# Two transformer blocks with a mixture of experts on one core: the overflow loop between the 16th and 17th expert, and expert outputs added to x in memory

## What is computed

```python
def hierarchical_moe(h, w_rg, b_rg, w_re, b_re, w_gate, w_up, w_down):
    ...
    expert_ids = g_idx[:, None] * EXPERTS_PER_GROUP + top_idx      # two experts a token
    combine = ...                                                  # its two weights
    out = jnp.zeros_like(tok)
    for e in range(N_EXPERTS):
        hid = jax.nn.silu(tok @ w_gate[e]) * (tok @ w_up[e])       # 1024 -> 256
        out = out + combine[:, e:e + 1] * (hid @ w_down[e])        # 256 -> 1024
    return out.reshape(b, s, d)
...
        x = x + gate_f * hierarchical_moe(h, ...)
    return rmsnorm(x, norm_final)
```

## Time and profile before

| | |
|---|---|
| median of 3 runs | 1525.57 us (1522.67 to 1530.29) |
| the profiled execution, its own time | 1524.17 us |
| its span in the trace | 1522.3 us |
| TensorE busy | 1376.1 us, 90% |
| VectorE busy | 713.2 us, 47% |
| ScalarE busy | 391.7 us, 26% |
| GpSimd busy | 298.3 us, 20% |
| moved by DMA | 249.11 MB, mean 164 GB/s |
| chain of waits that ended last | PE 75%, DMA 8%, DVE 6%, ACT 3%, issue 3% |

### The profile page before, as it was taken

The page is one execution under the profiler, slowest core; times in us unless marked ns, Lnnn a source line. Parts: engine busy times, 40 slices in busy tenths (PEclk is TensorE's granted clock), DMA queues, the critical chain, the costliest instruction groups (busy, mean ns, idle before and its releaser), DMA issues.

```text
span 1522.3 us, 17400 instructions
## 1 busy us (share of the span) xinstructions
PE 1376.1 (90%) x6971; PEld 1053.4 (69%) x6971; DVE 713.2 (47%) x937; ACT 391.7 (26%) x503; POOL 298.3 (20%) x280
## 2 busy tenths in 40 slices
PE   5999999999899999999979999977888959997872
PEld 4889888777788888888758887665666835554430
DVE  3324432365564554647461323287882436443234
ACT  5222544432432322223342222311112210000001
POOL 0500000001120201102000008045551113332212
PEclk9999999999999999999889999877877969999996
DMA  5222322534153453535022231000003979999964
GB/s 199 90 104 97 122 93 84 201 110 166 42 225 149 166 207 124 206 125 196 31 108 72 99 103 70 28 22 1 1 1 107 406 308 379 415 417 419 417 264 173
DMA packets 44261, 249.11 MB, mean 164 GB/s; under 512 B 10101, under 2 KB 10757, under 8 KB 17441
## 3 DMA queue, kind: packets, MB, share of 16 engines
q1 hardware_dynamic: 36514, 228.73, 39.2%
q0 software_dynamic: 7104, 17.35, 3.0%
q10 hardware_dynamic: 576, 2.10, 0.3%
HBM read 240.26 MB, written 17.06 MB: 169 GB/s over the span
## 4 chain that ended last, share of the span: by engine, by line
PE 75%; DMA 8%; DVE 6%; issue 3%; ACT 3%; SPq 2%; POOL 2%; POOLq 0%; ACTq 0%; DVEq 0%
PE ps L334 19%; PE ps L336 19%; PE ps L335 19%; DMA experts<-in_w_exp 6%; PE ps L2042 4%; PE ps L2060 2%; SPq L523 1%; PE ps L1938 1%; PE ps L1856 1%; PE ps L1666 1%; PE ps L288 1%; DVE raw L1157 1%; DMA arena<-h,arena 1%; DMA h<-experts 1%; DVE arena L1157 1%
## 5 line engine op out<-in xcount | busy, mean ns | idle before, releaser
L319 DVE TENSOR_TENSOR w_low<-raw,w_high 128x2048 fp32r<-128x2048 f32 x81 | 214.4, 2648 | 268.7 <-ACT w_high L315 268.7
L334 PE MATMUL ps<-u_high,w_high 128*128 128x512 f32 (+1 forms) x712 | 279.5, 392 | 0.0
L336 PE MATMUL ps<-u_high,w_low 128*128 128x512 f32 (+1 forms) x712 | 277.3, 389 | 0.0
L335 PE MATMUL ps<-u_low,w_high 128*128 128x512 f32 (+1 forms) x712 | 277.1, 389 | 0.0
L315 ACT ACTIVATE w_high<-raw 128x2048 fp32r<-128x2048 f32 x81 | 154.6, 1910 | 184.0 <-PE ps L336 153.3
L334 PEld LDWEIGHTS ps<-u_high,w_high 128*128 128x128 f32 (+1 forms) x712 | 132.9, 187 | 30.4 <-issue 1.7
L336 PEld LDWEIGHTS ps<-u_high,w_low 128*128 128x128 f32 (+1 forms) x712 | 132.9, 187 | 29.0
L335 PEld LDWEIGHTS ps<-u_low,w_high 128*128 128x128 f32 (+1 forms) x712 | 133.0, 187 | 28.2 <-issue 0.2
L334 PE MATMUL ps<-w_high,v_high 128*128 128x512 f32 x320 | 125.4, 392 | 0.0
L336 PE MATMUL ps<-w_high,v_low 128*128 128x512 f32 x320 | 125.2, 391 | 0.0
L335 PE MATMUL ps<-w_low,v_high 128*128 128x512 f32 x320 | 125.1, 391 | 0.0
(11 more groups left out here) (393 smaller groups left out, 1979.5 us busy)
## 6 DMA issues: line engine op xcount, KB each, us to landing
raw<-in_w SPq DMA_DIRECT2D x82, 1024.0 KB
experts<-in_w_exp SPq DMA_DIRECT2D x69, 1024.0 KB
arena<-in_w_exp SPq DMA_DIRECT2D x30, 1024.0 KB
arena<-in_w_ada SPq DMA_DIRECT2D x24, 1024.0 KB
gates<-arena POOLq DMA_DIRECT2D x16, 256.0 KB, 3.0
arena<-gates POOLq DMA_DIRECT2D x2, 2048.0 KB, 9.2
arena<-y SPq DMA_DIRECT2D x8, 512.0 KB, 6.8
x<-in_x SPq DMA_DIRECT2D x1, 2048.0 KB, 7.3
```

What stands on the lines that cost most here:

```text
L319: dve.tensor_tensor(WL[:, 1 - s, :], RAW[:, 1 - s, :], WH[:, 1 - s, :].bitcast(F32), ALU.subtract).then_inc(lo_ready, 1)
L334: pe.matmul(out, a[0], b[0], start=start, stop=False)
L335: pe.matmul(out, a[0], b[1], start=False, stop=False)
L336: return pe.matmul(out, a[1], b[0], start=False, stop=stop)
```

## The change

- The ring of slots gets one more place after expert 15: `place(b)` is b up to expert 15, and b + 1 from expert 16. The place between them (place 16, slot 2) is the overflow's.
- All 32 experts are written out. The run-time loop holds only overflow blocks (at least one turn) and stands on each engine between expert 15 and expert 16. It has one step semaphore with 11 steps a turn (`over_step`), tokens, transposed tokens and product banks that the neighbours don't use, and its own output tile.
- TensorE leaves the loop when the last turn's output is written. GpSimd issues expert 16's gather and the first overflow gather, then the outputs of experts 12 to 14, then enters the loop; before it goes on with expert 17's gather it waits for the overflow's scatter to land.
- ScalarE stores x to `y` (512 rows now) after `h2`. The scatters add to `y` in memory; each waits until the one before has landed, since both may touch one row. One index list serves gather and scatter. An additional scatter with an empty list stands before the loop.
- The last stage reads `y` back straight into x, four DMAs; no additions follow.

```diff
+OVER_AT = 16
+OVER_SLOT = OVER_AT % RING
+STEPS = 11
+def place(b):
+    return b if b < OVER_AT else b + 1
...
             def expert_weights(b):
-                slot, e = b % RING, t["w_exp"][b, :, :]
-                if b >= RING:
-                    sp.wait_ge(unit_done, M0 + b - RING + 1)
+                slot, e = place(b) % RING, t["w_exp"][b, :, :]
+                before = place(b) - RING
+                if before == OVER_AT:
+                    sp.wait_ge(over_step, STEPS * n + 10)
...
-            for b in range(RING, STATIC):
+            for b in range(RING, OVER_AT):
                 expert_weights(b)
             sp.wait_ge(route_d, 1)
...
             with sp.Fori(0, n) as j:
                 e = sp.value_load(EBI[0:1, bass.ds(j, 1)], min_val=0, max_val=N_EXP - 1)
-                sp.wait_ge(over_free, j + 1)
+                sp.wait_ge(over_step, STEPS * j + 10)
...
+            for b in range(OVER_AT, N_EXP):
+                expert_weights(b)
...
             for c in range(NC):
-                for k in range(2):
-                    sp.dma_start(YC[:, c, k, :], t["y"][S * k + P * c:S * k + P * c + P, :]).then_inc(yc_in[c], 16)
+                sp.dma_start(X[:, c, :], t["y"][P * c:P * c + P, :]).then_inc(yc_in[c], 16)
...
+            def x_row(c):
+                act.wait_ge(wo2_add, 5 + c)
+                act.dma_start(t["y"][P * c:P * c + P, :], X[:, c, :]).then_inc(x_out, 16)
...
             h2_row(3)
+            for c in range(NC):
+                x_row(c)
...
-            for c in range(NC):
-                dve.wait_ge(yc_in[c], 32)
-                link(dve.tensor_tensor(X[:, c, :], X[:, c, :], YC[:, c, 0, :], ALU.add))
-                dve.tensor_tensor(X[:, c, :], X[:, c, :], YC[:, c, 1, :], ALU.add).then_inc(fin_x, 1)
...
+            def scatter_rows(rows, index, signal):
+                pool.indirect_dma_start(halves_of_y, bass.IndirectOffsetOnAxis(ap=index, axis=0), rows, None,
+                                        bounds_check=2 * S - 1, oob_is_err=False, compute_op=ALU.add).then_inc(signal, 16)
...
+            def stored(b):
+                pool.wait_ge(y_out[b % 2], 16 * (b // 2) + 16)
+
+            def store(b):
+                pool.wait_ge(y_cp, b + 1)
+                if b:
+                    stored(b - 1)
+                else:
+                    pool.wait_ge(x_out, 16 * NC)
+                scatter_rows(YB[:, b % 2, :], IDX[:, b:b + 1], y_out[b % 2])
...
+                if b == OVER_AT:
+                    overflow()
+                elif 4 <= b and not OVER_AT < b < OVER_AT + 3:
+                    store(b - 4)
```

More of the change, by code:

```diff
@@ L51, with loads @@
 FAR = 8192
-STATIC = N_EXP - 1
-OVER_SLOT = STATIC % RING
+OVER_AT = 16
[3 more added lines that the diff above has]
+    return b if b < OVER_AT else b + 1
+def loads(b):
+    return sum(place(e) % RING == place(b) % RING for e in range(b + 1))
 NEG = -1.0e30
@@ L517, in expert_weights @@
             def expert_weights(b):
-                slot, e = b % RING, t["w_exp"][b, :, :]
-                if b >= RING:
-                    sp.wait_ge(unit_done, M0 + b - RING + 1)
+                slot, e = place(b) % RING, t["w_exp"][b, :, :]
+                before = place(b) - RING
+                if before == OVER_AT:
+                    sp.wait_ge(over_step, STEPS * n + 10)
+                    before = None
+                elif before > OVER_AT:
+                    before -= 1
+                if b >= RING and before is not None:
+                    sp.wait_ge(unit_done, M0 + before + 1)
                 for part in range(2):
@@ L523, in expert_weights @@
                     sp.dma_start(SLOTS[slot][:, w], e[:, w]).then_inc(gu_in[slot], 16)
-                if b >= RING:
-                    sp.wait_ge(m_down, b - RING + 1)
+                if b >= RING and before is not None:
+                    sp.wait_ge(m_down, before + 1)
                 sp.dma_start(SLOTS[slot][:, 2 * UNIT:], e[:, 2 * UNIT:]).then_inc(dn_in[slot], 16)
@@ L1588, in _ @@
+                gather(b, place(b) % 3, IDX[:, b:b + 1], xg_in[place(b) % 3])
+                if b == OVER_AT:
+                    overflow()
+                elif 4 <= b and not OVER_AT < b < OVER_AT + 3:
+                    store(b - 4)
+            for b in range(N_EXP - 4, N_EXP):
+                store(b)
             for c in range(NC):
@@ L2061, in down @@
                                          SLOTS[slot][:, w:w + HALF], start=k == 0, stop=k == 1)
-                last.then_inc(m_down if isinstance(b, int) else over_free, 1)
-            def loads(b):
-                return b // RING + 1
+                last.then_inc(m_down, 1)
             def down_static(b):
-                down(b, b % RING, b % 2, dn_base[b % RING] + 16 * loads(b))
-            x_tr(0, 0, 0, xg_in[0], 16)
-            for b in range(STATIC):
-                gate_up(b, b % RING, b % 2, b % 2, gu_base[b % RING] + 32 * loads(b))
-                x_tr(b + 1, (b + 1) % 3, (b + 1) % 2, xg_in[(b + 1) % 3], 16 * ((b + 1) // 3 + 1))
+                slot = place(b) % RING
@@ L2074, in _ @@
+            x_static(0)
+            for b in range(N_EXP):
+                if b == OVER_AT:
+                    pe.wait_ge(y_cp, b - 1)
+                    pe.wait_ge(ht_cp, b)
+                    overflow()
+                slot = place(b) % RING
+                gate_up(b, slot, b % 2, b % 2, gu_base[slot] + 32 * loads(b))
+                if b < N_EXP - 1:
+                    x_static(b + 1)
                 if b:
```

216 lines of the change are left out of this document (120 added, 96 removed).

## The result

The changed kernel takes **1567.72 us** (median of 4 runs, 1564.72 to 1568.27) beside 1527.66 (1522.67 to 1530.29) for the kernel before: a ratio of **1.0269, 95% interval 1.0248 to 1.0290**. It is 40 us slower; 1520.5 was predicted, and 1542 was the high end of the range. The profiled execution has a span of 1566.4 us against 1522.3.

The account below looks back on a forecast made before the run. TensorE for two thirds of the span, then expert weights at 8.43 us each: 1475.7 + 2 + 10.6 = 1488.3, last landing 1502.9, plus 15.1 gives span 1518.0, 1521.3 on the median's scale; said 1520.5, range 1507 to 1542.

Parts of the forecast that it names:

- Part 1: Expert stage, overflow moved to the middle: its 18 us hidden, last expert's gate and up weights at 1475.7.
- TensorE without a wait for weights after load 28 breaks part 1: Expert stage, sign against the hidden overflow: TensorE never waits for weights after load 28.
- part 4: Last weights to end: scatter chain free before, last landing 14.6 us after those weights, last stage 15.1 against 24.8.
- the overflow isn't hidden: Expert stage: TensorE over 25 us late at load 20, against 12 forecast; adds some 5 us; late TensorE's chance 0.03.
- The cover: Expert stage: the saturated second half, waiting on weights, hides the moved overflow's 18 us.
- Part 2: Storing x first: first gather late by 0 to 5 us, taken as +2; a landing past 1246 breaks it.
- Part 3: Adding scatters in the saturated stretch: 0.353 us more each, for 30 scatters +10.6 us (0 to 21).
- The first rival: Saturated stretch: adding scatters cost the queue nothing (0 to 4 us), time 1508 to 1515; chance 0.37.
- another rival: Saturated stretch: an adding row holds its DMA engine; at 1.2 us each, time 1547; chance 0.20, shared with serial chain.
- one over 9.3 the second: Expert stage: pitch of waited-for starts over 9.3 us, against 8.8 forecast, means an adding row holds its DMA engine.

Follow-up runs that it names:

- the two planes: Changed kernel with adding scatters into two tensors in turn, each waiting for the one two experts before, eight read-backs: 1536.44 us, ratio 1.0065.
- The adding half alone: Kernel before, overflow still at the end, with adding scatters each waiting for the one before, x stored first, four read-backs: 1565.68 us, ratio 1.0271.

## Why the prediction was wrong

**Part 1 (the overflow to the middle) was right in its sum.** Alone it gives 1515.4, with the last start at 1477.55 for 1475.7, and the wait for weights there that "TensorE without a wait for weights after load 28 breaks part 1" asked for. Two of its terms were too small: the turn took 15.6 us of TensorE (1342.61 to 1364.50 less 6.32) for 12.7, and the wait for expert 17's tokens was 13.4 for 5.3. Expert 17 so began at 1386.6, not 1372.5. The second was too small by the same misreading as in part 4: it priced a landing at 4.0 and a gather at 3.4, and under the stream they take 6.9 and 7.6. The rival "the overflow isn't hidden" was much nearer than its 0.03. Its limit was TensorE 25 us late at load 20, and there it was 24.7 us late (1399.23 against 1374.58); it waited for weights again from load 31 only, not from 22 to 26. The cover held with nothing to spare and 7 us of holes; that the sum came out is in part luck.

**Part 2 (x stored first)** was taken as 2 us. The first gather took 7.52 against 7.10 and landed at 1243.8, so it did not pass 1246. That cost some 0.4 us.

**Part 3 (adding costs the queue)** said 10.6 us for the adding, with a spread of 0 to 21. The account shows 14 to 16 in the queue that adds. The term was too small by 3 to 5 us and within its spread; the price per scatter came out at 0.45 to 0.52 us more, for 0.353. That it is the added read that costs this was argued and is not shown, since the count of bytes does not show that read. The Trainium skill's rule on the halved rate (Collectives: The Full Stack, "The bandwidth ceiling: the fold count and why AG ≠ RS ≠ AR") would make the extra as large as the 0.353 of one plain transfer. The trace agrees in size and is somewhat above. The first rival, a cheap scatter, falls. The prediction argued against it with "both sides are at their share of 1.02", but the profile has one share for an engine and does not part its two sides.

**Part 4 is where the prediction failed**: it put the wait of each scatter for the one before at nothing. The sentence is: "Before saturation ends the serial chain costs nothing: a scatter starts every 8.4 us and the longest plain one took 5.8." Three things in it were wrong.

**The landing was read from the wrong transfers.** The landing line under a group counts only transfers whose landing the profile could match. The transfer view by stretch says which those were (count, then median us to landing where there is one). The kernel before from 1300 to 1360, engines saturated, and from 1480 to 1500, the quiet end:

```profile
arena<-h,arena POOLq DMA_INDIRECT x10
y<-arena POOLq DMA_INDIRECT x9
...
y<-arena POOLq DMA_INDIRECT x2, 4.0
```

In the loaded stretch the profile has no landing for any scatter. The 4.0 is the middle of two landings from the end, 5.8 for the scatter at 1480 and 2.3 for the last; the "longest plain one" was the longer of two out of 33. The kernel with the overflow alone in the middle has matched ones from 1400 to 1450, with the same plain scatters under the same stream:

```profile
y<-arena POOLq DMA_INDIRECT x8, 6.9
arena<-h,arena POOLq DMA_INDIRECT x8, 7.6
```

The one gather beside streaming weights that the trace of before did time stood in the earlier trace rows: 7.10 us. I used that row for part 2 and not for part 4.

**The adding scatter under load was never priced.** The 3.5 us that I took was meant for the quiet end, and there it was a little low: the last two scatters landed after 4.8 and 3.7, and the read-back was issued at 1550.33, 16.3 us after the last expert's start, for 14.6. Under load a landing takes 8.3 in the median and up to 9.9, and the next issue starts 0.8 to 1.1 later.

**The pitch was held against the wrong limit**, the 8.4 us of the weights. Up to expert 19 TensorE goes at 6.32, and by being ahead it frees the slots that keep the queue full. A file of 7.4 us (plain) already makes TensorE late and empties the queue around the overflow; one of 10 (adding) is slower than the weights' 8.4 as well, so it sets the pace until the last weights are in.

The condition itself had been written down: "If a scatter's landing passes 8.4 us, the serial chain on GpSimd takes over with the same sign." That is what happened, and as the tail of another rival it had a part of 0.20 and a price that stopped at 1547. The sign "one over 9.3 the second" fits the pitch and names the wrong mechanism: no run shows a scatter that costs the engines the 1.2 us of that rival's price; they show 0.45 to 0.52 more than a plain one, and the two planes gave back most of the loss at the same cost in the engines.

The end of part 4 held: two scatters in file, no additions, 16.1 us for 15.1. Of that the last read-back took 0.7 more than its 7.65: it had landed 8.4 us after the first one's issue. The estimate of 6.8 by the fit in the Trainium skill (DMA: Bandwidth & Descriptors, "Anatomy of one DMA") was further off; that section gives the fit for transfers that GpSimd issues, and these are SP's. The 9 us gained in the last stage stand against some 60 for the file and the adding.

**The sum as it should have been**, by the ratios of the runs times 1525: overflow in the middle -12 (0.9921); plain scatters in file +26 (1.0089); last stage shorter and x stored -9 (1.0029); adding +37 (1.0269), of which some 14 is busy engines and the rest a longer file; together, before rounding, +41. Each step is measured on top of those before it; in another order they would come out otherwise.

## What to carry to other kernels

Before a wait for a DMA's landing is put between two steps of a loop, price that landing from a transfer that ran under the same load, and check by stretch that the view really timed such transfers. Compare landing plus issue with the shortest pitch at which the loop must run, not with the pitch of whatever bounds it now. If accumulating into memory needs order, spread it over two targets, so that each waits for the one before last; here that gave back 31 us of 40, and the kernel was still 0.65% slower than the one before. Plain scatters into separate rows, which need no order, and the overflow in the middle were the best here (0.8% faster).

## What the runs showed of the hardware

- Issuing an adding scatter of 128 rows of 2 KB takes GpSimd 1587 ns in the median, a plain one 1010.
- Its landing: 3.7 to 4.8 us beside little other traffic; under the full stream of weights 8.3 against 6.7. With half the weight bytes it is 5.0 in the median, with weight rows of half the length 7.4.
- The software queue counts 9360 packets in the changed kernel at the same bytes (17.36 MB), and 7184 with adding left out (17.35 MB). That is 2176 packets more for 34 scatters, 64 each, where a block has 128 rows. The adding half alone has 9216 against 7104 of the kernel before, 64 each for 33 scatters. Why 64, no run tells.
- An adding scatter keeps the DMA engines busy 0.45 to 0.52 us longer than a plain one (14 to 16 us for 31), at the same count of bytes.
- Weight rows of 4 KB in place of 8 KB keep the weights' queue busy 207 us in place of 199 for about the same bytes (82.2 and 81.8 MB).
